# Summing the squares of x by accumulating transfers, and moving h's low part two steps later, in a two-block transformer kernel

## The reference, cut to what matters

```python
def rms_norm(x, g):
    var = jnp.mean(x * x, axis=-1, keepdims=True)
    return x * lax.rsqrt(var + EPS) * g

def first_block(x, ...):                       # once
    z = rms_norm(x, norm_mix) @ w_in           # windowed attention, neighbourhood attention, gates
    x = x + merged @ w_out
    x = x + square(relu(rms_norm(x, norm_mlp) @ w_up)) @ w_down
    return rms_norm(x, norm_final)

def second_block(x, ...):                      # two layers
    for l in range(2):
        x = x + 0.5 * swiglu(rms_norm(x, ffn1_norm[l]), ...)
        z = rms_norm(x, mix_norm[l]) @ w_in[l] # sliding attention, short convolution
        x = x + concat(attn_out, conv_out) @ w_out[l]
        x = x + 0.5 * swiglu(rms_norm(x, ffn2_norm[l]), ...)
    return rms_norm(x, final_norm)
```

## Time and profile before

| | |
|---|---|
| median of three runs | 2504.01 us |
| the profiled execution's own time | 2501.46 us |
| its span | 2499.3 us |
| TensorE (PE) busy | 2427.9 us, 97% of the span |
| VectorE (DVE) busy | 1822.6 us, 73% |
| ScalarE (ACT) busy | 1269.4 us, 51% |
| GpSimd (POOL) busy | 195.3 us, 8% |
| 16 DMA engines | 263.76 MB in all, mean 106 GB/s |
| mean granted TensorE clock | 0.989 of full speed |

### The profile page before, as it was taken

One profiled execution on the slowest core, in us unless ns is written; L12 is line 12 of the kernel. 1 busy time (PEld: TensorE's weight loads), 2 busy tenths in 40 slices (PEclk: granted clock), 3 DMA queues, 4 the chain that ended last, 5 costly groups with the idle time before them and its releaser, 6 DMA issues.

```text
span 2499.3 us, 36547 instructions
## 1 busy us (share of the span) xinstructions
PE 2427.9 (97%) x14620; PEld 2158.8 (86%) x14620; DVE 1822.6 (73%) x2639; ACT 1269.4 (51%) x2023; POOL 195.3 (8%) x199
## 2 busy tenths in 40 slices
PE   9999998999979999999999999989999999999999
PEld 7878888999859999978889999889999788899998
DVE  7742477777679878675688777788877766887874
ACT  6677354444354544357454444554444465544443
POOL 2231010000030000012100000100000121000001
PEclk9999999999999999999999999999999999999999
DMA  7655442333322333236323333222332363233331
GB/s 204 151 124 126 118 135 85 102 102 100 100 71 79 107 102 102 68 106 156 109 84 95 102 102 102 98 89 93 102 102 77 109 152 110 85 102 102 102 101 68
DMA packets 103640, 263.76 MB, mean 106 GB/s; under 512 B 9648, under 2 KB 12976, under 8 KB 103088
## 3 DMA queue, kind: packets, MB, share of 16 engines
q1 hardware_dynamic: 94848, 233.57, 29.8%
q0 software_dynamic: 8624, 27.86, 5.5%
HBM read 234.56 MB, written 2.19 MB: 95 GB/s over the span
## 4 chain that ended last, share of the span: by engine, by line
PE 73%; DVE 12%; ACT 6%; issue 5%; DMA 3%; POOL 1%; SPq 0%; POOLq 0%; DVEq 0%; ACTq 0%
PE bank L1107 12%; PE bank L1108 12%; PE bank L1109 12%; PE bank L1155 12%; PE bank L1156 11%; PE bank L1157 11%; DVE w_raw_lo L1600 2%; DVE slot_lo L1600 2%; DVE x L1864 1%; ACT w_hi L1315 1%; PE bank L1171 1%; PE bank L1186 1%; DMA w_raw<-w_out_dram 1%; DVE rms_inv L1760 1%; ACT z L1303 1%
## 5 line engine op out<-in xcount | busy, mean ns | idle before, releaser
L1361 ACT ACTIVATE slot_hi<-slot_raw 128x1024 fp32r<-128x1024 f32 (+1 forms) x396 | 365.2, 952 | 144.3 <-DVE slot_raw L1646 115.8
L1600 DVE TENSOR_TENSOR slot_lo<-slot_raw,slot_hi 128x1024 fp32r<-128x1024 f32 (+1 forms) x396 | 427.1, 1100 | 4.1 <-ACT slot_hi L1361 4.1
L1155 PE MATMUL bank<-hs_hi,slot_hi 128*128 128x256 f32 x1504 | 426.1, 283 | 0.1
L1157 PE MATMUL bank<-hs_hi,slot_lo 128*128 128x256 f32 x1504 | 426.2, 283 | 0.0
L1156 PE MATMUL bank<-hs_lo,slot_hi 128*128 128x256 f32 x1504 | 426.1, 283 | 0.0
L1107 PE MATMUL bank<-act_hi,w_hi 128*128 128x512 f32 x960 | 380.3, 396 | 7.8 <-DVE w_raw_lo L1600 7.8
L1108 PE MATMUL bank<-act_lo,w_hi 128*128 128x512 f32 x960 | 380.2, 396 | 0.0
L1109 PE MATMUL bank<-act_hi,w_raw_lo 128*128 128x512 f32 x960 | 374.6, 390 | 0.0
L1155 PE MATMUL bank<-h_hi,slot_hi 128*128 128x256 f32 x1128 | 322.8, 286 | 39.2 <-DVE slot_lo L1600 35.8
L1379 ACT ACTIVATE part_a<-bank 128x256 f32<-128x256 f32 x188 | 71.8, 382 | 531.0 <-PE bank L1157 530.4
L1864 DVE SCALAR_TENSOR_TENSOR x<-bank,x 128x512 f32<-128x512 f32 x280 | 192.3, 687 | 191.3 <-PE bank L1109 190.0
(11 more groups left out here) (263 smaller groups left out, 4345.7 us busy)
## 6 DMA issues: line engine op xcount, KB each, us to landing
slot_raw<-ffn_wg_dram SPq DMA_DIRECT2D x88, 512.0 KB, 4.1
slot_raw<-ffn_wu_dram SPq DMA_DIRECT2D x88, 512.0 KB, 4.1
w_raw<-ffn_wd_dram SPq DMA_DIRECT2D x88, 512.0 KB, 3.7
w_raw<-w_in_dram SPq DMA_DIRECT2D x67, 512.0 KB, 3.6
w_lo<-w_raw POOLq DMA_DIRECT2D x43, 512.0 KB, 4.7
slot_raw<-w_up_dram SPq DMA_DIRECT2D x32, 512.0 KB, 4.4
w_raw<-w_down_dram SPq DMA_DIRECT2D x32, 512.0 KB, 3.6
w_raw<-w_out_dram SPq DMA_DIRECT2D x24, 512.0 KB, 3.7
```

The costliest lines, as they stand in the source:

```text
L1155: engine.matmul(to, slot_hi[:, g % 2, slot, lhs], hi, start=opens, stop=False, skip_group_check=True)
L1157: product = engine.matmul(to, slot_lo[:, g % 2, slot, lhs], hi, start=False, stop=closes, skip_group_check=True)
L1361: engine.activation(span_of(slot_hi, n, name), span_of(slot_raw, n, name), ACT.Copy).then_inc(signals["s_hi"].s, 1)
L1600: engine.tensor_tensor(lo, value, hi.bitcast(F32), ALU.subtract).then_inc(signals[event].s, 1)
```

## The change

For stages 1 to 7 (in the diff, `v` is DVE's queue and `pool` is POOL's):

- ACT squares tile 0 into `square_sum` and tile 1 into a second sum, `square_odd`. Tiles 2 to 7 are squared into a buffer `z` as before, but POOL doesn't add them: it issues a transfer from `z` to the sum with `accum_op=ALU.add`, even tiles into `square_sum`, odd ones into `square_odd`. A transfer into a sum waits for the one before it into the same sum.
- A new job `square_fold`, five slots after tile 7's, adds the two sums on DVE, once the last transfer into each has landed.
- `sum_split` is put seven slots after tile 7's instead of four.
- A new job `h_rest` takes DVE's part of `h_tile` and stands two slots behind it; ACT's part stays. In stage 0 it follows at once.

The sums for FINAL and for stage 0, and `scaled_sum`, are made as before. `square_odd` lies where `sum_lo` lies.

```diff
-        "h_tile": ("h_hi", "h_lo"), "gain_product": ("gain_product",),
+        "h_tile": ("h_hi",), "h_rest": ("h_lo",), "gain_product": ("gain_product",),
...
     def square(self, s, m):
-        if m == 0:
+        if m == 0 or m == 1 and 0 < s < FINAL:
             self.add("square_first", (s, m))
+        elif 0 < s < FINAL:
+            self.add("square_add", (s, m), None, self.z(f"square_added{m % 2}", (s, m)))
+            self.sig[f"square_added{m % 2}"].will((s, m))
+            if m == KT - 1:
+                self.later(5, "square_fold", s)
         else:
             self.add("square" if s > 0 else "square_zero", (s, m), None, self.z("square_sum", (s, m)))
 
     def norm_tile(self, s, m):
         self.add("h_tile", (s, m))
+        self.later(2, "h_rest", s, m)
         self.square(s, m)
...
         if m == KT - 1 and s in SPLIT_SUMS:
-            self.later(4, "sum_split", s)
+            self.later(7, "sum_split", s)
...
-                    square(key, square_sum[:, :], m, signals["squared"])
+                    square(key, (square_sum, square_odd)[m][:, :], m, signals["squared"])
...
-                elif job == "h_tile":
+                elif job == "h_rest":
                     s, m = key
                     v.wait_ge(*done("h_hi", key))
...
+                elif job == "square_fold":
+                    v.wait_ge(*done("square_added0", (key, KT - 2)))
+                    v.wait_ge(*done("square_added1", (key, KT - 1)))
+                    engine.tensor_tensor(square_sum[:, :], square_sum[:, :], square_odd[:, :], ALU.add).then_inc(signals["square_sum"].s, 1)
...
+                elif job == "square_add":
+                    s, m = key
+                    pool.wait_ge(*done("squared", key))
+                    if m > 3:
+                        pool.wait_ge(*done(f"square_added{m % 2}", (s, m - 2)))
+                    engine.dma_start((square_sum, square_odd)[m % 2][:, :], z[zs % Z_RING][:, :], accum_op=ALU.add).then_inc(signals[f"square_added{m % 2}"].s, 16)
```

More of the change, by code:

```diff
@@ L155 @@
         "fetch": (), "split_first": ("first_hi", "first_lo"), "split_v": ("w_hi", "w_lo_v"), "split_hi": ("w_hi",), "split_rest": ("w_lo_v",), "split_g": ("w_hi", "w_minus"), "k_step": (), "k_last": (),
-        "h_tile": ("h_hi", "h_lo"), "gain_product": ("gain_product",),
-        "square_first": ("squared",), "square_zero": ("squared", "square_sum"), "square": ("squared", "square_sum"), "square_last": ("squared",),
+        "h_tile": ("h_hi",), "h_rest": ("h_lo",), "gain_product": ("gain_product",),
+        "square_first": ("squared",), "square_zero": ("squared", "square_sum"), "square": ("squared", "square_sum"), "square_add": ("squared",), "square_fold": ("square_sum",), "square_last": ("squared",),
         "scaled_first": ("scaled_squared",), "scaled": ("scaled_squared", "scaled_sum"),
@@ L204, in add @@
             if name not in self.OF_SINKS or SINK[key[0]] is not None:
-                self.sig[name].will(key)
+                self.sig[name].will((key, KT - 1) if job == "square_fold" else key)
         if r is not None and job not in ("k_step", "k_last"):
@@ L234, in run @@
             return
-        if job in ("sum_split", "split_rest") or job.startswith("s_") and len(key) == 1:
+        if job in ("sum_split", "split_rest", "square_fold") or job.startswith("s_") and len(key) == 1:
             key = key[0]
@@ L374, in dense_first @@
             self.add("h_tile", (0, k))
+            self.add("h_rest", (0, k))
             self.add("split_first", k)
@@ L836, in two_blocks @@
             sbuf("to_sum_lo", [P, 24 * TOKENS * 4], mybir.dt.uint8, on)
+            with ExitStack() as sums:
+                square_odd = sbuf("square_odd", [P, TOKENS], F32, sums)
             sum_lo = sbuf("sum_lo", [P, TOKENS], F32R, on)
@@ L904, in two_blocks @@
             signals[f"w_added{i}"] = signal(f"w_added{i}", 16)
+        for i in range(2):
+            signals[f"square_added{i}"] = signal(f"square_added{i}", 16)
         out_stored = signal("out_stored", 16)
@@ L1037, in two_blocks @@
                 x_of["now", key] = r
-            elif job in ("h_tile", "square", "square_first", "square_last", "output_gain", "output_gain_last") and key[0] > 0:
+            elif job in ("h_tile", "square", "square_add", "square_first", "square_last", "output_gain", "output_gain_last") and key[0] > 0:
                 x_of[key] = x_of["now", key[1]]
@@ L1407, in scalar_program @@
                         act.wait_ge(*done("s_out", h_until[s][1][0]))
-                    square(key, square_sum[:, :], m, signals["squared"])
-                elif job in ("square", "square_zero", "square_last"):
+                    square(key, (square_sum, square_odd)[m][:, :], m, signals["squared"])
+                elif job in ("square", "square_add", "square_zero", "square_last"):
                     square(key, buffer(zs), key[1], signals["squared"])
```

## The result

| | us, median (lowest to highest, runs) |
|---|---|
| before, same chip | 2502.85 (2500.72 to 2505.83, 5) |
| changed kernel | 2515.66 (2513.34 to 2522.17, 5) |
| ratio, 95% interval | 1.0055 [1.0038, 1.0072] |
| predicted | 2496.7, range 2490.0 to 2506.0 |

The change costs 12.8 us, 0.5%, where a gain of 7.3 was forecast. The profiled execution, the slowest of the five, took 2522.17 us, its span 2520.4.

The account below looks back on a forecast made before the run. It took DVE's queue to set the pace for TensorE where x is renewed. Terms of +2.4 (stages 1, 4, 7), -2.8 (5), -4.5 (2) and -2.4 (3, 6) gave -7.3 on 2504.0: 2496.7 us, range 2490 to 2506.

Parts of the forecast that it names:

- Collisions (part 1): Down projections: with POOL's additions gone, w_raw_lo returns to 1.22 us, saving DVE 1.09 us per weight unit.
- 4.9 us of DVE for a unit: Down projections: DVE's work per weight unit falls to 4.9 us, below TensorE's 5.4, so TensorE's waits there vanish.
- the walk ahead of it: Stage 2: following DVE's queue put the last residual at 712.1 instead of 717.01; the stage gains 4.5 us.
- h_lo two slots later (part 2): Down projections: odd tiles' h_lo behind w_raw_lo hides DVE's 0.79 us wait for h_hi; no effect in out projections.
- The size of a landing (part 3): End of each stage: the last square's 256 KB transfer lands after 3.2 us, bounds 2.9 and 4.7.
- The row of 8.3 us: Earlier trace: slowest accumulating 512 KB transfer, cited as showing that accumulating beside fetches can take nearly twice the median.
- the rule that a stage loses what a landing takes longer: All seven stages: 7 us lost per us of longer landing; at 4.25 us nothing of the gain is left.
- the -2.4 forecast: Stages 3 and 6: 1.8 us of TensorE waits go, 0.45 come back; 1.2 us gain taken for each.
- instead of 2.8: Stage 5: the last residual comes earlier, at 1607.1, so hs_lo starts 2.8 us earlier than 1619.27, a 2.8 us gain.
- Stages 1, 4, 7: After the last residual, landing and fold delay hs_lo from 366.98 to 367.8: loss 0.8 us each, 2.4 for three.
- The clock: After gaps TensorE runs at 1.2 GHz; changed gap lengths could cost or save 1.5 us per stage, plus or minus 3.
- transfers land too late: Rival, chance 0.12: landings late beside SyncE's 512 KB fetch, DVE and ACT both waiting; at 5.3 us, 2511 us total.

Follow-up runs that it names:

- squares_alone: The changed kernel with h_lo back right behind h_hi, so only the accumulating transfers are left of the change: 2515.48 us, 1.0043 against before.
- after_again: The changed kernel itself, unaltered, run and profiled once more on another chip: 2518.93 us, 1.0059 against before.
- far_later: The changed kernel with SyncE's 1 MB table load put 24 slots later in stages 3 and 6: 2506.07 us, 1.0007 against before.
- h_alone: The kernel before with only h_lo moved two slots behind h_hi; POOL still adds the squares: 2495.74 us, 0.9968 against before.
- last_by_transfer: h_alone with only the eighth square of stages 1 to 7 added by an accumulating transfer, no fold: 2505.34 us, 1.0012 against before.
- idle_transfers: h_alone plus 42 accumulating 256 KB transfers, awaited only for the buffer's release: 2506.89 us, 1.0014 against before.
- two_by_pool: The changed kernel with each stage's last two squares added by POOL, the first four transfers and the fold kept: 2498.05 us, 0.9973 against before.
- last_by_dve: h_alone with the eighth square of stages 1 to 7 added by DVE instead of POOL: 2494.22 us, 0.9960 against before.

## Why the prediction was wrong, step by step

**Collisions (part 1).** Right where POOL has no `scaled` additions: w_raw_lo takes 1216 ns in stage 3 and 1.22 us in stage 5. Wrong in stage 2. There the `scaled` additions stay, and h_lo's new place puts w_raw_lo and h_lo beside them. DVE in the changed kernel, from the last residual to `norm_twice`, and its w_raw_lo in squares_alone:

```profile
720.88 0.68 DVE L1880 SCALAR_TENSOR_TENSOR x<-bank,x 128x512 f32<-128x512 f32 x1
722.30 2.06 DVE L1611 TENSOR_TENSOR w_raw_lo<-w_raw,w_hi 128x1024 fp32r<-128x1024 f32 x1 [0.73 <-ACT w_hi L1326]
724.29 2.19 DVE L1628 SCALAR_TENSOR_TENSOR h_lo<-x,gain_product,h_hi 128x512 fp32r<-128x512 f32 x1
...
733.22 0.68 DVE L1785 TENSOR_SCALAR z<-bank 128x512 f32<-128x512 f32 x1
```

```profile
720.10 1.21 DVE L1611 TENSOR_TENSOR w_raw_lo<-w_raw,w_hi 128x1024 fp32r<-128x1024 f32 x1
```

I had counted 4.9 us of DVE for a unit. The residuals of the last two odd tiles are 7.7 us apart (713.19 to 720.88), no less than the 7.3 of before, and the last residual comes 1.6 us earlier by the offset, not 4.9. From there to `norm_twice` it is 12.34 us, forecast 12.2. So the part behind the last residual was right and the walk ahead of it wrong: -1.3 instead of -4.5. Each part alone gains more in this stage (-3.2 and -3.4) than both together.

**h_lo two slots later (part 2).** Right. In stages 3 and 6 TensorE's waits for w_raw_lo are gone, in stage 5 the last residual comes 4.4 us earlier by the offset, forecast 4.45. By itself it is worth 9 us. In stage 2 it spoils the first part, as said.

**The size of a landing (part 3).** 3.2 us was taken, and alone on the queues it is 3.2 (stages 1, 2, 4 and 5; 3.3 in 7). The step that failed is to take it everywhere. I had looked at the fetch of 512 KB beside it, and found that it has moved most of its bytes by then. I had not listed what else SyncE issues at that point of the order; in stages 3 and 6 it is 1 MB. The row of 8.3 us was the warning, and the rival that used it priced 5.3 us for all stages, where it is 3.2 in five and, in the first trace, 9.4 and 8.5 in two (10.7 and 8.6 in after_again). By the rule that a stage loses what a landing takes longer, 6.2 and 5.3 more are 11.6 us; the two went from the -2.4 forecast to +11.1 and +13.4. This term is 13.5 and 15.8 of the 22.5 us between forecast and traces; far_later gives back 12.9. The rule of 1 us per us was wrong there too, and that the two numbers lie close is luck: up to a landing of about 5 us these stages lose 0.2 to 1.8 us against h_alone (last_by_transfer, far_later), and beyond it more than the landing grows. From far_later to after_again the landings are 5.9 and 3.3 us longer, the stages 8.9 and 5.5. The Trainium skill's fit ("DMA: Bandwidth & Descriptors", section "Anatomy of one DMA — SWDGE (gpsimd) path") gives an estimate of 2.6 us for 256 KB; the least landing of an accumulating transfer of that size is 3.2 here, so the trace does not agree.

**The wait for the transfer before.** It had no term at all. The kernel never has two transfers into one sum under way together, so POOL holds the eighth until the sixth has landed. POOL in stage 5, and DVE behind it:

```profile
1618.42 0.86 POOL L2033 DMA_DIRECT2D square_odd<-z  x1 [1.68 <-DMA square_odd<-z]
1624.39 0.86 POOL L2033 DMA_DIRECT2D square_odd<-z  x1 [2.90 <-DMA square_odd<-z]
...
1620.52 0.68 DVE L1880 SCALAR_TENSOR_TENSOR x<-bank,x 128x512 f32<-128x512 f32 x1
1627.70 0.69 DVE L1768 TENSOR_TENSOR square_sum<-square_sum,square_odd 128x512 f32<-128x512 f32 x1 [4.50 <-DMA square_odd<-z]
1631.57 1.22 DVE L1611 TENSOR_TENSOR hs_lo<-h_mixed,hs_hi 128x1024 fp32r<-128x1024 f32 x1
```

ACT's square ended at 1622.49, the issue starts at 1624.39, 1.9 us behind it; where nothing holds it, an issue starts 0.3 to 0.4 behind. Residual to hs_lo is 11.05 us where I had 9.4 and before had 7.72. In after_again the sixth landed in time (issue 0.50 behind the square) and the same stretch is 9.64, close to the forecast. So this wait comes and goes, and it is not all of the gap: stage 5 gained 0.3 and 1.2 instead of 2.8. Tiles of a down projection come 2.1 and 2.6 us apart there, and the landings of the fourth to the sixth took 3.3 to 6.0 us.

**Stages 1, 4, 7.** The sign was right and the size half: +1.4 to +2.4, forecast +0.8. DVE of stage 1 against the earlier trace rows, with POOL's issue:

```profile
363.80 0.68 DVE L1880 SCALAR_TENSOR_TENSOR x<-bank,x 128x512 f32<-128x512 f32 x1
372.63 1.22 DVE L1611 TENSOR_TENSOR hs_lo<-h_mixed,hs_hi 128x1024 fp32r<-128x1024 f32 x1
379.92 3.35 DVE L1776 RECIPROCAL rms_inv<-z 128x512 f32<-128x512 f32 x1 [0.29 <-ACT z L1439]
...
366.18 0.86 POOL L2033 DMA_DIRECT2D square_odd<-z  x1 [5.12 <-ACT z L1314]
```

Residual to hs_lo: 8.83, forecast 8.5, before 7.41; the 0.3 is the 0.42 between the end of ACT's square (365.76) and the issue. hs_lo to the reciprocal: 7.29, as before. The other half is ahead of it: ACT waited 1.77 us for w_raw's fetch before the last residual, and that came 0.3 late by the offset (0.1 in after_again, with a wait of 1.50), not 0.3 early. That fetch took 4.95 and 4.72 us in the two traces, each beside a square's transfer, and 3.85 before and 3.69 in h_alone, which has no such wait.

**The clock.** The gap of stage 3 costs its own time and then some at the lower level (0.63 from 1099 to 1103); mean granted clock 0.985 after, 0.989 before. In the 14 us behind the gap, with no wait longer than before, TensorE falls behind by another 1.2 us in stage 3 and 0.8 in stage 6 (2.1 and 0.8 in after_again). That is within the 3 us either way that I had left for it, but those were for the gaps of stages 1, 2, 4, 5 and 7. The range does not follow from its own bounds, either: a landing of 2.9 us with 3 us of clock gives 2491.6 and a landing of 4.7 gives 2507.2, where I wrote 2490 and 2506.

Summed against the two traces of the changed kernel, on average over them but for the first: stages 3 and 6 forecast -2.4, measured +11.1 and +13.4; stage 2, 3.2 off; stage 5, 2.0; stages 1, 4 and 7, 2.6. The rival "transfers land too late" had the right mechanism and sign, with a chance of 0.12. Its 2511 had the wrong places: 2.1 us in each of seven stages.

Open: how the loss of 11 to 13 us in stages 3 and 6 divides between the wait at the fold and the late w_in fetch. TensorE's own waits name the sum (7.00 and 6.10 us) and, unlike in h_alone and idle_transfers, none for the reciprocal behind it; but with the sum in time the fetch would have cost some of it, as the 2.5 and 4.1 us of idle_transfers say. Open too: what makes a landing of 7.7 one of 8.5 to 10.7, and why DVE's stage 4 loses more than stage 1 in the first trace and not in the second.

## What to carry to other kernels

A landing on the path is priced at its worst place, not at its usual one: for each place list every transfer that any queue issues in the 10 us around it, the rare ones (a table once per layer) first, and ask what both queues behind the landing hold. Early parts of a sum may go by transfer without a wait for them (two_by_pool), but they are not free, and here they brought nothing in total: the fastest kernel of all, by its median ratio, has none (last_by_dve, 0.9960), and transfers that nobody waited for cost 11 us, 3 of them through POOL's queue (idle_transfers). The last part is best added by the engine that reads the sum next (last_by_dve). A change of order that costs nothing can be worth more than the clever half of a change, and the two can spoil each other: test each alone.

## What the runs showed of the hardware

A 256 KB accumulating transfer within the SBUF took 3.2 us from issue to landing when alone, up to 6.9 beside fetches of 512 KB (two_by_pool), 5.2 to 5.6 beside a 1 MB load, 7.3 to 7.7 where two of them lay beside it and 8.2 to 10.7 in the changed kernel's two traces, where four more went ahead. The load took 5.5 to 6.3 us in the kernel before and 7.4 to 9.4 in the changed one (one of h_alone's took 7.5 with no transfer of a square).

An addition of POOL stretches h_lo and w_raw_lo, which read all their operands from the SBUF, by up to 1.0 and 1.1 us (beside a `scaled` addition h_lo by 1.5, to 2.2). It does not stretch the residual, which reads a bank of PSUM and x: 0.68 us beside an addition, as everywhere. In the kernel before:

```profile
709.67 0.68 DVE L1864 SCALAR_TENSOR_TENSOR x<-bank,x 128x512 f32<-128x512 f32 x1
709.57 1.34 POOL L2019 TENSOR_TENSOR square_sum<-square_sum,z 128x512 f32<-128x512 f32 x1 [3.04 <-ACT z L1303]
```

POOL's issue of a transfer stretches none of those seen: w_raw_lo starts at 1084.61 under the issue of 1084.52 and takes 1.22.
